# Bringing the softmax sums' inverses to all partitions: TensorE transposes and a PSUM copy, or a pass through DRAM

## The reference

```
s = einsum(qn, k_nope) + einsum(qr, k_rope)
p = softmax(s * MLA_SCALE, axis=-1)
o = einsum('bhqk,bkhd->bqhd', p, v)
mixed = concat([o_mla * silu(gate_mla), ...])
```

## Time and profile before

| | |
|---|---|
| median of 3 runs | 750.37 us (746.06 to 754.07) |
| profiled execution | 750.29 us, span of the trace 748.5 us |
| TensorE matmul | 721.3 us busy, 96% |
| VectorE | 408.9 us, 55% |
| ScalarE | 311.9 us, 42% |
| POOL | 287.6 us, 38% |
| DMA | 96.14 MB, mean 128 GB/s |
| granted TensorE clock | 0.987 of full speed |

### The profile page before, as it was taken

One profiled execution on the slowest core, in us unless ns is written; L12 is line 12 of the kernel. 1 busy time (PEld: TensorE's weight loads), 2 busy tenths in 40 slices (PEclk: granted clock), 3 DMA queues, 4 the chain that ended last, 5 costly groups with the idle time before them and its releaser, 6 DMA issues.

```text
span 748.5 us, 14234 instructions
## 1 busy us (share of the span) xinstructions
PE 721.3 (96%) x5784; PEld 606.4 (81%) x5784; DVE 408.9 (55%) x718; ACT 311.9 (42%) x520; POOL 287.6 (38%) x290
## 2 busy tenths in 40 slices
PE   8999999999999999999999789889989999999996
PEld 6998878878888888888888588788788988888885
DVE  5855877376575543026175757758656654333232
ACT  6554444334423432233223545555554654232321
POOL 3223226366556512122400255553555854322320
PEclk9999999999999999999999889999999999999999
DMA  7613021001122233230235886786886035564441
GB/s 255 183 26 89 28 97 57 30 31 40 63 72 87 73 114 107 92 88 26 63 144 180 249 240 207 230 225 184 264 233 194 1 109 180 176 196 158 139 151 56
DMA packets 65389, 96.14 MB, mean 128 GB/s; under 512 B 6161, under 2 KB 43537, under 8 KB 65330
## 3 DMA queue, kind: packets, MB, share of 16 engines
q1 hardware_dynamic: 53856, 65.34, 30.3%
q10 hardware_dynamic: 11474, 29.96, 10.6%
HBM read 59.30 MB, written 35.00 MB: 126 GB/s over the span
## 4 chain that ended last, share of the span: by engine, by line
PE 76%; DVE 8%; DMA 7%; ACT 4%; POOL 2%; issue 2%; SPq 0%; ACTq 0%; DVEq 0%; POOLq 0%
PE psum L78 20%; PE psum L80 19%; PE psum L79 19%; PE psum L1535 4%; DMA spread_scratch<-a_spread_second 3%; DVE a_top L2082 2%; PE psum L1374 2%; DMA a_turned_lo_third<-spread_scratch 2%; ACT a_weights L1982 2%; POOL a_turned_lo_third L1895 2%; PE psum L1254 1%; DVE g_state L1062 1%; DVE a_weights L2055 1%; DMA a_turned_lo<-spread_scratch 1%; PE psum L1404 1%
## 5 line engine op out<-in xcount | busy, mean ns | idle before, releaser
L78 PE MATMUL psum<-h_hi,z_w_hi 128*128 128x512 f32 x376 | 152.4, 405 | 0.0
L80 PE MATMUL psum<-h_hi,z_w_lo 128*128 128x512 f32 x376 | 146.8, 390 | 0.0
L79 PE MATMUL psum<-h_lo,z_w_hi 128*128 128x512 f32 x376 | 146.6, 390 | 0.0
L78 PEld LDWEIGHTS psum<-h_hi,z_w_hi 128*128 128x128 f32 x376 | 70.6, 188 | 15.9 <-issue 0.7
L80 PEld LDWEIGHTS psum<-h_hi,z_w_lo 128*128 128x128 f32 x376 | 70.6, 188 | 15.4
L79 PEld LDWEIGHTS psum<-h_lo,z_w_hi 128*128 128x128 f32 x376 | 70.7, 188 | 14.0 <-issue 0.7
L1982 ACT ACTIVATE a_weights<-psum,a_bias,mla_q_scale 128x1024 f32<-128x1024 f32 (+1 forms) x48 | 51.0, 1062 | 64.9 <-DVE a_bias L2085 64.9
L805 POOL TENSOR_TENSOR z_w_lo<-z_w_raw,z_w_hi 128x1024 fp32r<-128x1024 f32 x17 | 41.0, 2411 | 94.5 <-ACT z_w_hi L501 92.4
L78 PE MATMUL psum<-o_w_hi,o_m_hi 128*128 128x512 f32 x184 | 72.6, 394 | 0.0
L80 PE MATMUL psum<-o_w_hi,o_m_lo 128*128 128x512 f32 x184 | 72.3, 393 | 0.0
L79 PE MATMUL psum<-o_w_lo,o_m_hi 128*128 128x512 f32 x184 | 72.2, 392 | 0.0
(11 more groups left out here) (281 smaller groups left out, 1656.5 us busy)
## 6 DMA issues: line engine op xcount, KB each, us to landing
z_w_raw<-in_w_z_dram SPq DMA_DIRECT2D x17, 512.0 KB, 3.6
n_x_in<-in_x_dram SPq DMA_DIRECT2D x12, 512.0 KB, 4.3
gates_scratch<-z_gate ACTq DMA_DIRECT2D x24, 256.0 KB, 2.1
spread_scratch<-a_weights ACTq DMA_DIRECT2D x12, 512.0 KB, 5.0
spread_scratch<-a_spread_second ACTq DMA_DIRECT2D x12, 512.0 KB, 6.6
a_turned_lo<-spread_scratch SPq DMA_DIRECT2D x24, 256.0 KB, 5.2
o_x_in<-in_x_dram SPq DMA_DIRECT2D x12, 512.0 KB, 3.6
out_dram<-o_y ACTq DMA_DIRECT2D x11, 512.0 KB, 3.2
```

Source lines behind the costliest of these rows:

```text
L78: nc.tensor.matmul(out, a_hi, b_hi, start=first, stop=False)
L79: nc.tensor.matmul(out, a_hi, b_lo, start=False, stop=False)
L80: return nc.tensor.matmul(out, a_lo, b_hi, start=False, stop=last)
```

## The change

The share columns go through DRAM. A new scratch tensor `share_dram` has a row pair of 2 x 128 values for each of the 24 pairs. When both shares of a pair are ready, SP stores them there, 128 partitions by two columns (`store_shares`), and then loads the 256 values to all 128 partitions (`load_shares`), into the place in `keep.mixed` which the pair's output will take (`mixed_of`). One semaphore, `share_passed`, counts both, and each waits for the one before. `gather(p)` is then a single product that reads its second factor from its own destination. The transposes in `output`, its wait for the shares, the copy and `share_row` are gone. For the first 18 pairs the store stands ahead of the pair's spread loads and the load behind them; the last six pairs stand behind the loads of the output weights. In the last head the inverse is taken one step after the exponential, with a wait ahead of it, where it was two.

```diff
-        self.share_row = rest("a_share_row", [P, 2, PAIR])
...
+        def mixed_of(p):
+
+            return keep.mixed[:, p // (2 * TB), (p % (2 * TB)) * PAIR:(p % (2 * TB) + 1) * PAIR]
...
+            def store_shares(p):
+                if p:
+                    sp.wait_ge(share_passed, 32 * p)
+                sp.wait_ge(share_ready, 2 * p + 2)
+                sp.dma_start(share_dram[p].rearrange("n t -> t n"), share[:, 2 * p:2 * p + 2],
+                             allow_slow_non_contiguous=True).then_inc(share_passed, 16)
+
+            def load_shares(p):
+                sp.wait_ge(share_passed, 32 * p + 16)
+                sp.dma_start(mixed_of(p), share_dram[p].rearrange("n t -> (n t)").partition_broadcast(P))\
+                  .then_inc(share_passed, 16)
...
             for p in range(SPREAD_PAIRS):
                 count = keys_of(2 * p)
+                store_shares(p)
                 for n in range(2):
                     sp.wait_ge(spread_stored[n], 16 * p + 16)
...
                       .then_inc(spread_loaded[p % 3], 16)
+                load_shares(p)
                 if p % 2:
                     load_rope(2 * p // TILES + 1, p % (TILES // 2) // 2)
...
                     sp.dma_start(keep.mix_first[:, :, :], mix_dram[:, :, 0:P].rearrange("a p t -> p a t"))\
                       .then_inc(mix_loaded, 16)
+            for p in range(SPREAD_PAIRS, PAIRS):
+                store_shares(p)
+                load_shares(p)
...
             def gather(p):
-                h, t = p // (2 * TB), (p % (2 * TB)) * PAIR
                 dve.wait_ge(output_done, p + 1)
-                nc.vector.tensor_copy(share_row[:, p % 2, :], psum[:, 6 + p % 2, PAIR:]).then_inc(gathered, 1)
-                dve.wait_ge(gathered, 2 * p + 1)
-                nc.vector.tensor_tensor(keep.mixed[:, h, t:t + PAIR], psum[:, 6 + p % 2, :PAIR],
-                                        share_row[:, p % 2, :], ALU.mult).then_inc(gathered, 1)
+                dve.wait_ge(share_passed, 32 * p + 32)
+                nc.vector.tensor_tensor(mixed_of(p), psum[:, 6 + p % 2, :PAIR], mixed_of(p), ALU.mult).then_inc(gathered, 1)
...
                 if 1 <= m <= LAST_HEAD:
                     transpose(m - 1)
+                if LAST_HEAD < m <= STEPS:
+                    dve.wait_ge(exp_done, m)
+                if 1 <= m <= STEPS:
                     take_share(m - 1)
...
                 if LAST_HEAD <= m - TURN_LAG < STEPS:
                     tile = m - TURN_LAG
-                    dve.wait_ge(exp_done, tile + 1)
-                    take_share(tile)
...
             def values(p):
                 _, first, count = QUERY_TILES[(2 * p) % TILES]
                 if p >= 2:
-                    pe.wait_ge(gathered, 2 * p - 2)
+                    pe.wait_ge(gathered, p - 1)
...
             def output(p):
                 h = p // (2 * TB)
-                pe.wait_ge(share_ready, 2 * p + 2)
                 pe.wait_ge(latent_lo_ready, p + 1)
-                for n in range(2):
-                    nc.tensor.transpose(psum[:, 6 + p % 2, PAIR + n * P:PAIR + (n + 1) * P],
-                                        share[:, 2 * p + n:2 * p + n + 1].broadcast_to([P, P]), ident[:, :])
                 product(nc, psum[:, 6 + p % 2, :PAIR], keep.w_v_hi[:, h * P:(h + 1) * P], keep.w_v_lo[:, h * P:(h + 1) * P],
                         latent_hi[:, p % 2, :], latent_lo[:, p % 2, :]).then_inc(output_done, 1)
...
+        share_dram = scratch("share_scratch", (PAIRS, 2, P), F32)
```

More of the change, by code:

```diff
@@ L1771, in portion, with phase_mla_attend @@
     return slice((m % 2) * keys_of(m), (m % 2 + 1) * keys_of(m))
-def phase_mla_attend(nc, cx, block, front, rope_dram, gates_dram, mix_dram, spread_dram, w_out_dram, w_out_loaded, gate_loaded, mix_loaded, psum,
-                     ident, keep):
+def phase_mla_attend(nc, cx, block, front, rope_dram, gates_dram, mix_dram, spread_dram, share_dram, w_out_dram, w_out_loaded, gate_loaded, mix_loaded,
+                     psum, ident, keep):
     with ExitStack() as mem:
@@ L1794, in phase_mla_attend @@
         spread = [weights[:, 2, :], spread_second[:, :]]
-        rest, q_rope, share_row = keep.rest, keep.q_rope, keep.share_row
+        rest, q_rope = keep.rest, keep.q_rope
         top = rest("a_top", [P, STEPS])
@@ L1807, in phase_mla_attend @@
         share_ready = sem("a_share_ready")
+        share_passed = sem("a_share_passed")
         transposed = sem("a_transposed")
@@ L1908, in _ @@
                 if i == 4:
-                    pool.wait_ge(gathered, 3 * TILES + 2)
+                    pool.wait_ge(gathered, SPREAD_PAIRS + 1)
                     multiply(of_heads, heads_gates).then_inc(first_step, 1)
@@ L2302, in weight_gates @@
                 nc.gpsimd.tensor_tensor(mix[s][:, :, :], mix[s][:, :, :], gate[s][:, 4:8, :], ALU.mult).then_inc(gated, 1)
-            pool.wait_ge(attend.gathered, 2 * PAIRS)
+            pool.wait_ge(attend.gathered, PAIRS)
             nc.gpsimd.memset(minus_half[:, :], -0.5).then_inc(half_set, 1)
@@ L2496, in hymba_encoder_kernel @@
         first_mix_loaded = cx.semaphore("first_mix_loaded")
-        attend = phase_mla_attend(nc, cx, block, front, rope_dram, gates_dram, mix_dram, spread_dram, dram["w_out"], w_out_loaded,
+        attend = phase_mla_attend(nc, cx, block, front, rope_dram, gates_dram, mix_dram, spread_dram, share_dram, dram["w_out"], w_out_loaded,
                                   first_gate_loaded, first_mix_loaded, psum, ident, keep)
```

## The result

The changed kernel takes 937.15 us (median of 4 runs, 932.91 to 939.03) against 750.17 for the kernel before in the same comparison: a ratio of 1.249, 95% interval 1.241 to 1.257. It is 187 us slower. The forecast was 749, no change that can be measured, with a range of 739 to 764; the result lies 173 us above its upper end.

The account below looks back on a forecast made before the run. It saw three near limits in turn: DMA latency, a VectorE/ScalarE loop, TensorE. 750.3 us minus 4.3 of gain plus 2.9 of longer transits gave 748.9, forecast 749, range 739 to 764.

Parts of the forecast that it names:

- 4.3 us of gain: Attention stage: time saved by dropping transposes and copies where they count; lower end 0, upper end 9.0 us.
- The 1.8 us of the last head's eight pairs: TensorE-bound tail, pairs 16 to 23: dropped transposes save 0.22 us for each of eight pairs, 1.8 us.
- the 1.8 + 0.7 in the spread heads: Copy off the chain for four pairs, 1.8 us; three more pairs in the full TensorE stretch 495 to 511 us, 0.7 us.
- The price of the store: 256 pieces of 4 bytes per pair: 0.3 us of DMA engine time, from above 1.8; landing taken as 2.1 us.
- the upper end of 11.7: Last head: one store-and-load trip taken as 5.1 us, from above 11.7 with two landings of 5.4.
- The seven on the chain: Seven DMA transits of spread weights, 415 to 540 us: 0.4 us longer each, 2.9 in all; ends nothing and 12.6.
- The traffic rival: Spread transits: 4-byte pieces cost like the ACT queue's packets, 1.8 us more per transit, 761.1 us in all; chance 0.14.
- the string: Last head: six trips one after another on SP delay the last gather if each exceeds 6.8 us; 756.2 to 778.4; chance 0.12.
- 6 T - 40.7: Last head's loss in us from six trips of T us each, between 572.5 and the last gather at 613.2.
- at most 8.7: SP's wait for the previous share load before short pairs 4, 10, 16: cost nothing, at most 3 x 2.9 = 8.7 us.
- a trip of 8.7 us: Last head: trip estimate with 1.8 us on each of two landings, from the skill page; time 760.4 us.
- 778: String rival's upper end in the last head: a price of 29.5 us, time 778.4 us.

Follow-up runs that it names:

- the removal alone: Kernel before without transposes, copy and DRAM trips; the product takes another tile, so the division is left out: 747.19 us, ratio 0.997.
- the store-only kernel: Kernel before plus the first 18 of the 4-byte stores, no share loads, nothing waiting for them: 829.02 and 842.05 us in two runs.
- the unstrung kernel: Changed kernel with the same stores and loads, but each pair's share load leaves one pair later, behind the next pair's spread loads: 843.38 us, ratio 1.129.
- the kernel with pieces apart: Changed kernel with its 256 pieces of 4 bytes each in 64 bytes of DRAM of its own, loads reading an input tensor: 756.89 us, ratio 1.012.
- the one-column kernel: Changed kernel storing only one column, 128 pieces of 4 bytes side by side, loads reading an input tensor: 893.83 us, ratio 1.195.

## Why the prediction was wrong, point by point

**TensorE and VectorE.** Right in kind, about half in size. Predicted 4.3 us of gain; the removal alone shows 3.1 in the profiled spans (748.5 to 745.4) and about 2 in the runs. The 1.8 us of the last head's eight pairs measured 1.7. Of the 1.8 + 0.7 in the spread heads 1.8 came.

**The price of the store: the step that failed.** The prediction bounded the store's time on the engines, 0.3 to 1.8 us a pair; on idle engines it was less still, 9 ns for each of 16 pieces on an engine, 0.14 us. It then took the landing from a 0.5 KB load, 2.1 us, from above 5.4. A load of small rows from DRAM is no neighbour of small writes into DRAM, and the measured landing on idle engines is 8.0 us, outside the range on its upper side. The text said that writes may be dearer and then put that into the engines' time alone. With 8.0 and 4.4 to 5.2 for the load a trip is 12.5 to 13.1 us, above the upper end of 11.7.

**The transits.** The seven on the chain were to grow by 0.4 us (0.42 in the sum, for 2.9), at most 1.8. In the median the spread stores of the store-only kernel went from 5.0 to 10.3 and from 6.6 to 10.7 us, and on the chain of the unstrung kernel they reach 16.9. The mechanism was taken as a share of the engines' time; what the runs show is that beside such stores others land late, on another queue too, though the small stores themselves take the engines almost no time (9 ns a piece, where it could be read). The traffic rival had the right direction and about a seventh of the size (11 us of loss, 79 and 92 measured).

**SP's queue.** The prediction saw the string in the last head only, and put a chance of 0.12 on it; its formula 6 T - 40.7 gives 34 to 38 us for the measured T, and the last head lost 37.1. For the first 18 pairs it looked at one wait, that for the load of the pair before, at a landing that it believed short. In fact the trips set the pace there too: 138.9 us lost, against at most 8.7. The cut string bought back 94 us. But with a landing of 1.6 us (and loads of 3.1 in place of 4.4 to 5.2) the same string costs little: the kernel with pieces apart is at 757 with it, 9.6 us over before. So the string is an amplifier; that the pieces lie close together is the cause.

**The rule that spoke against the change.** The Trainium skill, "DMA: Bandwidth & Descriptors" (Rules for kernel authors, Specifications), has a strided last dimension cut into one descriptor per element and a read-modify-write below 512 B. The trace agrees with the first: 256 packets for the 256 elements. The second no run here shows. A read-modify-write for each piece, if there is one, can't be the price by itself: 4-byte pieces 64 bytes apart are under that size too, and land in 1.6 us. The same page's HBM access of 2 us at high load (Latency and other measured facts) gave a trip of 8.7 us as an estimate; measured were 12.5 and more with the engines nearly idle.

**The range and the chances.** 0.26 stood on slower, and the range's upper end of 764 left out even the upper end that the text itself had worked out, 778. Both ends of an operation that no row shows belong in the range when a whole queue waits behind it.

**What stays open.** Why close pieces make a store land late, and why others' writes land late with it, no run here shows; 16 pieces in 64 bytes cost 7 to 8 us and 8 cost 3, which isn't in proportion. Two readings fit every landing in the table: pieces that fall into one stretch of DRAM wait for one another, or they do so when they come from different DMA engines, of which more meet in a stretch the closer the pieces lie. No run separates them, and none shows how long that stretch is. Nor was it tried whether writes within SBUF do the same. Loads of a KB that close pieces had just written also took longer (4.4 to 5.2 us) than loads of an input's KB, even behind a store of close pieces (2.9 to 3.2 in the one-column kernel), and than loads of a KB written in rows (3.0); why is open too.

## What to carry to other kernels

Before a transfer is called hidden, price its landing, not its bytes or the engines' time, and when its form is in no row of the trace (here small writes into DRAM), run it alone first. Don't store pieces of 4 or 8 bytes side by side in DRAM: space them (a pitch of 32 bytes was enough here), or turn the data first so that it goes out in whole rows (128 bytes here). Don't let a shared DMA queue wait for a transfer that it has just issued; and ask first what the removal alone would bring, here 2 us, before building what replaces it.

## What the runs showed of the hardware

- A 1 KB store in 256 pieces landed in 1.6 or in 8.0 us, by its pieces' addresses alone (table above), with 9 ns a piece on the engines in the slow case.
- 18 stores of the slow form, waited for by nothing, made a kernel 79 to 92 us slower: 512 KB stores from another queue landed in 10.3 and 10.7 us in place of 5.0 and 6.6.
- The busy share of the DMA engines doesn't tell this: 0.81 at 146 GB/s with the small stores, about 0.8 at 235 GB/s without. Share and rate have to be read together.
- Two stores of one queue, 128 pieces each at a pitch of 8 bytes, issued 0.4 us apart, landed one after the other, in 3.1 and 6.3 us.
- A load of 128 rows from one and the same KB of DRAM, just written in close pieces, took 4.4 to 5.2 us on idle engines, 28.6% of 16 x 4.9 us for 144 packets or 156 ns each in one of them, where the prediction had 67 ns. It took 3.1 us in the median from an input tensor and 3.0 from a KB written in rows of 128 bytes.
